# A third row pair in the seven-product form, and a new order of units, in the output product of a fused encoder layer

## The chip, the cores and the metric

The kernel runs on one core of a Trainium2 chip, in one launch. The metric is the device time of that core in microseconds (us). The engines that matter here are TensorE (PE in the profile, with its weight loads as PEld), VectorE (DVE), ScalarE (ACT) and the DMA queue that SyncE feeds (SPq). They run in parallel, each takes its own instructions strictly in order, and they meet only at semaphores.

## The reference

One layer of a hybrid encoder on 256 rows (tokens) of width 2048 in float32. The stage that is changed is the third line, `merged @ w_out`, a 256x2048 by 2048x2048 product that is added to `x`:

```
y_conv = conformer_conv_branch(...)          # ends in h @ w_conv_out
y_mla  = mla_branch(...)                     # ends in o @ w_mla_out
merged = gates[:, :, 0, :] * y_conv + gates[:, :, 1, :] * y_mla
x = x + merged @ w_out[l]
x = x + memory_cross_attention(rms_norm(x, norm_mem_g[l]), rms_norm(mem, mem_norm_g[l]), ...)
x = x + squared_relu_mlp(rms_norm(x, norm_ffn_g[l]), w_ff1[l], w_ff2[l])
```

## The kernel before

**Precision.** Each float32 operand is split into a rounded "high" part and the rest, the "low" part. A block product is three matmuls: high by high, high by low, low by high. For a block of activations of 128 rows of K by 128 tokens, against 512 columns of weights, that is three matmuls of 128x512 (`product`).

**Units.** Weights come in units of two K blocks by 512 columns (512 KB). A ring of four raw slots (`raw`) and a ring of four split slots (`w_both`, high and low) carry them. For unit u, SyncE loads the raw slot once the low part of unit u-4 is made (`load`). ScalarE makes the high part (`hi`, 128x1024) once the load has landed and TensorE has released unit u-4 (`used`). VectorE makes the low part (`lo`, 128x1024) after `hi`. TensorE then runs the unit. In the loops of ScalarE and VectorE over k, the unit that is split is k + LEAD with LEAD = 3, and everything else in step k stands around it. A plain unit is four block products, 12 matmuls.

**Seven for eight.** The 2048 output columns are taken as two chunk pairs (p = 0 and 1, 1024 columns each), K as eight row pairs of two blocks. For one row pair, one pair of chunks and the two token halves, the plain way takes 2 x 2 x 2 = 8 block products. Two units of the same row pair (the "left" unit, chunk 0, and the "right" unit, chunk 1) can instead be taken in seven products, in the manner of Strassen and Winograd. The left unit then carries two products, the right unit one, and the other four run later from sums of weight blocks and sums of activation blocks. VectorE makes the weight sums from both raw slots (`w_sums`, three instructions that each wait for the one before). ScalarE splits off their high part in two halves (`ws_high`), VectorE the low part (`ws_low`, two halves). There is one `w_sum` buffer, so each row pair's sums wait for the low parts of the one before. Of the right unit only the second half is split (`hi_second`, `lo_second`). The sums of activations are made once, from the turned merged rows (`h_sums`, `h_low`), and serve both chunk pairs. The later products run behind unit 13 and behind unit 14 of the 16.

**Order around the stage.** The list `FF2_ORDER` gives (chunk, first K block) of each unit; `LEFT` and `RIGHT` are the positions of the left and right units, so that before the change two row pairs of eight, at positions 7, 8 and 11, 12, take seven products. The convolution output product (`U_COUT`, c = 2 and 3) runs before the stage. In it the merged rows of the first three chunks are turned (transposed on TensorE, `turn`) and split (`turn_out`, `turn_low`). The fourth is turned behind unit 3 of pair 0. In pair 1 TensorE turns the new `xres` behind units 1 and 12. A turn takes 8 small matmuls.

Of the kernel before, what the change touches and what calls it, by code (L numbers as in the profile page):

```python
# [211 lines left out]
def build(nc, x, mem, positions, norm_mix_g, w_in, b_gate, conv_w, conv_b, conv_ln_g, conv_ln_b,  # L212
# [9 lines left out]
    with ExitStack() as ctx:  # L222
# [75 lines left out]
        ws_hi = ((ws_a0_hi, ws_b0_hi), (ws_a1_hi, ws_b1_hi))  # L298
        ws_lo = ((ws_a0_lo, ws_b0_lo), (ws_a1_lo, ws_b1_lo))
# [389 lines left out]
        def _(act):  # L689
# [273 lines left out]
            for c in range(2, CH):  # L963
                for k in range(UPC):
# [3 lines left out]
                    if c == 2 and k == 4:  # L968
                        h_high(2)

            def out_squares(c):
# [3 lines left out]
                chunk_squares(sq_res, xres[:, :, NC * c:NC * (c + 1)], c, SS_MEM + TT * c)  # L975

            for p in range(2):
                for k in range(FF2_UNITS):
                    if k == 12:
                        y_out(OUT, p, 0)  # L980
                    if k + LEAD in RIGHT:
# [1610 lines left out]
```

## Time and profile before

| | |
|---|---|
| Time, median of 3 runs | 1596.12 us (1596.04 to 1596.23) |
| Profiled execution: its time, its span | 1596.36 us, 1594.1 us |
| Busy over the span | PE 99%, PEld 84%, DVE 82%, ACT 56% |
| Chain that ended last | PE 98% |
| In pair 0 of the stage (755 to 799 us) | PE 44.0 of 44 us, DVE 35.8, ACT 22.3 |
| In pair 1 of the stage (799 to 843 us) | PE 44.0 of 44 us, DVE 36.6, ACT 25.8 |

The span is the time from the first to the last instruction; the run's own time is 2.3 us longer. The duration of a matmul in the trace (389 ns) is a latency. Matmuls overlap, and their spacing is what a row of them costs. The same holds of VectorE and ScalarE to a smaller degree: an instruction of 1.22 us is followed by the next after 1.14 us.

### The profile page before, as it was taken

Reading aid. Unit: us, or ns where it says so; the run is one execution under the profiler, and the core shown is the slowest. Engines: PE = TensorE matmul, PEld = TensorE weight load, DVE = VectorE, ACT = ScalarE, POOL = GpSimd, SP = SyncE. Lnnn points to the kernel's source line nnn. Section 1 sums busy time; section 2 is a strip of 40 time slices with the busy share of each in tenths; the row PEclk is TensorE's granted clock in tenths of the full one; section 3 lists DMA queues with packets and bytes.
Section 4 is the critical chain, followed back from the end, with each engine's and each line's share of the span. In section 5 each row is a group of like instructions: output and inputs, shape, how many; then the busy total and the mean of one; then the engine's idle time right before and its main releaser. Section 6 shows DMA issues by size and latency. Waiting matters only on the chain.

```text
span 1594.1 us, 22178 instructions
## 1 busy us (share of the span) xinstructions
PE 1582.9 (99%) x7915; PEld 1343.4 (84%) x7915; DVE 1299.3 (82%) x1741; ACT 900.2 (56%) x1133; POOL 94.5 (6%) x174
## 2 busy tenths in 40 slices
PE   9999999999999999999999999999999999999997
PEld 8888888888888888888888888888888888888886
DVE  5588999999998998786887787886779676968687
ACT  6444456555555556754566666455655565546655
POOL 6500010000000000000000000000000000000001
PEclk9999999999999999999999999999999999999999
DMA  7666655655555666657664676888678867987694
GB/s 254 203 187 186 194 158 178 174 181 172 182 177 174 209 200 185 197 177 249 212 195 145 179 230 186 279 258 291 181 256 267 266 217 219 286 259 237 207 293 147
DMA packets 169581, 336.68 MB, mean 211 GB/s; under 512 B 10377, under 2 KB 23297, under 8 KB 169089
## 3 DMA queue, kind: packets, MB, share of 16 engines
q1 hardware_dynamic: 164608, 324.84, 64.4%
q0 software_dynamic: 4864, 10.80, 3.1%
q8 instruction: 50, 0.82, 0.2%
q14 instruction: 27, 0.22, 0.0%
q10 hardware_dynamic: 32, 0.01, 0.0%
HBM read 326.16 MB, written 2.10 MB: 206 GB/s over the span
## 4 chain that ended last, share of the span: by engine, by line
PE 98%; DVE 0%; ACT 0%; issue 0%; ACTq 0%; POOL 0%; POOLq 0%; DVEq 0%
PE ps L2508 15%; PE ps L1937 12%; PE ps L1939 12%; PE ps L1938 12%; PE ps L2217 9%; PE ps L2215 9%; PE ps L2216 9%; PE ps L2510 7%; PE ps L1950 1%; PE ps L2126 1%; PE ps L2335 1%; PE ps L2121 1%; PE ps L2104 1%; PE ps L2106 1%; PE ps L2105 1%; PE ps L2160 1%
## 5 line engine op out<-in xcount | busy, mean ns | idle before, releaser
L695 ACT ACTIVATE w_both<-raw 128x1024 fp32r<-128x1024 f32 x524 | 553.2, 1059 | 498.7 <-PE ps L1939 178.5
L1188 DVE TENSOR_TENSOR w_both<-raw,w_both 128x1024 fp32r<-128x1024 f32 x524 | 637.3, 1222 | 201.6 <-ACT w_both L695 199.9
L2508 PE MATMUL ps<-a_both,w_both 128*128 128x512 f32 x1024 | 321.6, 395 | 0.0
L1937 PE MATMUL ps<-w_both,a_both 128*128 128x512 f32 (+1 forms) x636 | 251.4, 395 | 0.1
L1939 PE MATMUL ps<-w_both,a_both 128*128 128x512 f32 (+1 forms) x636 | 247.1, 388 | 0.0
L1938 PE MATMUL ps<-w_both,a_both 128*128 128x512 f32 (+1 forms) x636 | 246.9, 388 | 0.0
L2510 PEld LDWEIGHTS ps<-a_both,w_both 128*128 128x128 f32 x1024 | 192.4, 188 | 45.4
L1249 DVE SCALAR_TENSOR_TENSOR acc<-hconv,cwk,acc 128x256 f32<-128x256 f32 x464 | 201.1, 486 | 7.7 <-PE ps L2160 7.6
L2510 PE MATMUL ps<-a_both,w_both 128*128 128x256 f32 x1024 | 201.2, 278 | 0.0
L2215 PE MATMUL ps<-w_both,c_hi 128*128 128x512 f32 x414 | 161.4, 390 | 0.0
L2216 PE MATMUL ps<-w_both,c_hi 128*128 128x512 f32 x414 | 161.1, 389 | 0.0
L2217 PE MATMUL ps<-w_both,c_lo 128*128 128x512 f32 x414 | 161.1, 389 | 0.0
L2508 PEld LDWEIGHTS ps<-a_both,w_both 128*128 128x128 f32 x1024 | 156.2, 189 | 0.3
L1939 PEld LDWEIGHTS ps<-w_both,a_both 128*128 128x128 f32 x636 | 119.4, 188 | 24.5
L1937 PEld LDWEIGHTS ps<-w_both,a_both 128*128 128x128 f32 x636 | 119.5, 188 | 23.2 <-DVE a_both L1209 0.3
L1938 PEld LDWEIGHTS ps<-w_both,a_both 128*128 128x128 f32 x636 | 119.6, 188 | 22.5
L2217 PEld LDWEIGHTS ps<-w_both,c_lo 128*128 128x128 f32 x414 | 77.7, 188 | 16.3
L2216 PEld LDWEIGHTS ps<-w_both,c_hi 128*128 128x128 f32 x414 | 77.7, 188 | 16.0
L2215 PEld LDWEIGHTS ps<-w_both,c_hi 128*128 128x128 f32 x414 | 77.7, 188 | 15.7
L1797 DVE TENSOR_TENSOR t_lo<-t_raw,t_hi 128x2048 fp32r<-128x2048 f32 x31 | 71.0, 2291 | 12.9 <-ACT t_hi L1090 12.7
L1090 ACT ACTIVATE t_hi<-t_raw 128x2048 fp32r<-128x2048 f32 x31 | 59.1, 1907 | 3.0 <-DVE t_raw L1792 3.0
L675 POOL DMA_DIRECT2D xres<-m_sum x7 | 8.4, 1197 | 820.0 <-DVE xres L1631 820.0
(418 smaller groups left out, 2208.4 us busy)
## 6 DMA issues: line engine op xcount, KB each, us to landing
raw<-in_w_ff_dram SPq DMA_DIRECT2D x225, 512.0 KB, 4.6
raw<-in_w_in_dram SPq DMA_DIRECT2D x137, 512.0 KB, 4.2
t_raw<-in_w_ff_dram SPq DMA_DIRECT2D x31, 1024.0 KB, 7.2
raw<-in_w_mla_out_dram SPq DMA_DIRECT2D x32, 512.0 KB, 4.3
raw<-in_w_conv_out_dram SPq DMA_DIRECT2D x32, 512.0 KB, 4.5
raw<-in_w_out_dram SPq DMA_DIRECT2D x32, 512.0 KB, 4.4
raw<-in_w_ukv_dram SPq DMA_DIRECT2D x16, 512.0 KB, 3.8
raw<-in_w_xkv_dram SPq DMA_DIRECT2D x16, 512.0 KB, 3.8
```

The costliest lines, as they stand in the source:

```text
L695: act.activation(whi[:, s, :], raw[:, s, :], ACT.Copy).then_inc(hi_ready, 1)
L1188: dve.tensor_tensor(wlo[:, s, :], raw[:, s, :], whi[:, s, :].bitcast(F32), ALU.subtract).then_inc(lo_ready, 1)
L1249: ins = dve.scalar_tensor_tensor(out=to, in0=h[:, tap:tap + SEQ], scalar=cwk[:, tap:tap + 1], in1=to, op0=ALU.mult, op1=ALU.add)
L1797: dve.tensor_tensor(t_lo[j % SLOTS][:], t_raw[j % SLOTS][:], t_hi[j % SLOTS][:].bitcast(F32), ALU.subtract).then_inc(t_lo_ready, 1)
L1937: pe.matmul(sum_, x_hi[:, k0 + k, tok], w_hi, start=(first and k == 0), stop=False)
L1938: pe.matmul(sum_, x_hi[:, k0 + k, tok], w_lo, start=False, stop=False)
L1939: mm = pe.matmul(sum_, x_lo[:, k0 + k, tok], w_hi, start=False, stop=(last and k == kts - 1))
L2215: pe.matmul(ps[:, bank, :], x_hi, w_hi, start=first, stop=False, skip_group_check=True)
L2216: pe.matmul(ps[:, bank, :], x_hi, w_lo, start=False, stop=False, skip_group_check=True)
L2217: return pe.matmul(ps[:, bank, :], x_lo, w_hi, start=False, stop=last, skip_group_check=True)
L2508: pe.matmul(both, whi[:, s, cols[n]], a_both[:, :, k0 + k, :], start=(first and k == 0), stop=False)
L2510: mm = pe.matmul(ps[:, b0 + b + n, 0:SEQ], wlo[:, s, cols[n]], a_hi[:, k0 + k, :], start=False, stop=(last and k == 1))
```

## The change

A third row pair takes the seven-product form in both chunk pairs. A new list `OUT_ORDER` replaces `FF2_ORDER` for this stage; left units stand at 4, 8 and 11, right units at 5, 9 and 12. `sum_high` and `sum_low` say at which step k the high and low parts of the weight sums are made. The third row pair's activation sums come from new code (`h3_sums`, a high and a low part) in the convolution output product, its weight sums get buffers in the idle `a_both` region, and a scratch of squares moves to another region. The convolution's own pair keeps the old list.

```diff
@@ -137,6 +137,12 @@
              (1, 10), (0, 12), (0, 2), (1, 2), (0, 14), (1, 12), (1, 14))
 FF2_UNITS = len(FF2_ORDER)
 LEFT, RIGHT = (7, 11), (8, 12)
+OUT_ORDER = ((0, 6), (0, 8), (1, 6), (1, 8), (0, 0), (1, 0), (0, 10), (1, 10), (0, 2),
+             (1, 2), (0, 12), (0, 4), (1, 4), (0, 14), (1, 12), (1, 14))
+OUT_LEFT, OUT_RIGHT = (4, 8, 11), (5, 9, 12)
+OUT_WS_HIGH = (2, 6, 10)
+OUT_WS_LOW = {2: (0, 1), 3: (0, 0), 6: (1, 1), 7: (1, 0), 10: (2, 1), 11: (2, 0)}
+OUT_PLANS = ((OUT_ORDER, OUT_LEFT, OUT_RIGHT, OUT_WS_HIGH, OUT_WS_LOW),) * 2
 ONES_BANK, LAST_BANK = 4, 5
 FF2_BANKS = ((2, 0), (2, 6))
 V_BANK, K_BANK = 4, 6
@@ -168,6 +174,16 @@
 TURN_MRG = {(2, 1): (0,), (2, 6): (1,), (3, 3): (2,)}


+def sums_before(p, m):
+
+    return 3 * m + (6 + 9 * p if p >= 0 else 0)
+
+
+def halves_before(p, m):
+
+    return 2 * m + (4 + 6 * p if p >= 0 else 0)
+
+
 def pair_of(n):

     return (n + 1) % 2
@@ -244,6 +260,8 @@
         sq_mem = at(o + KS + KS // 2, "sq_mem", [P, TT, NC])
         fin = at(o, "fin", [P, TT, D])
         fin_g = at(o + KS, "fin_g", [P, D])
+        ws_a2_hi, ws_b2_hi, ws_a2_lo, ws_b2_lo = (
+            at(o + at_byte, f"ws_third{n}", [P, 2 * NC], F32R) for n, at_byte in enumerate((8192, 12288, 24576, 28672)))
         sq_fin = at(o + KS + nbytes([P, D]), "sq_fin", [P, TT, NC])

         o = c_base = cursor[0]
@@ -295,8 +313,10 @@
...
-        ws_hi = ((ws_a0_hi, ws_b0_hi), (ws_a1_hi, ws_b1_hi))
-        ws_lo = ((ws_a0_lo, ws_b0_lo), (ws_a1_lo, ws_b1_lo))
+        ws_hi = ((ws_a0_hi, ws_b0_hi), (ws_a1_hi, ws_b1_hi), (ws_a2_hi, ws_b2_hi))
+        ws_lo = ((ws_a0_lo, ws_b0_lo), (ws_a1_lo, ws_b1_lo), (ws_a2_lo, ws_b2_lo))
+        h3_hi = at(o + 12288, "h3_hi", [P, 4, P], F32R)
+        h3_sum, h3_lo = at(o + 14336, "h3_sum", [P, 4, P]), at(o + 14336, "h3_lo", [P, 4, P], F32R)
@@ -516,7 +538,7 @@
             sp.wait_ge(h_made, 4)
             sp.dma_start(xres[:], x_v).then_inc(res_landed, 16)
             for p in range(2):
-                for i, (c, k) in enumerate(FF2_ORDER):
+                for i, (c, k) in enumerate(OUT_PLANS[p][0]):
                     n = 2 * p + c
                     load(U_WOUT + FF2_UNITS * p + i, 0, w_out[:, k:k + 2, NC * n:NC * (n + 1)])
             for hp in range(2):
@@ -967,18 +989,21 @@
...
+                    if c == 2 and k == 7:
+                        act.wait_ge(h3_made, 5)
+                        act.activation(h3_hi[:], h3_sum[:], ACT.Copy).then_inc(h3_hi_ready, 1)
...
-                chunk_squares(sq_res, xres[:, :, NC * c:NC * (c + 1)], c, SS_MEM + TT * c)
...
+                chunk_squares(sq_out, xres[:, :, NC * c:NC * (c + 1)], c, SS_MEM + TT * c)
+
+            for p, (_, _, right, sum_high, _) in enumerate(OUT_PLANS):
                 for k in range(FF2_UNITS):
                     if k == 12:
                         y_out(OUT, p, 0)
-                    if k + LEAD in RIGHT:
+                    if k + LEAD in right:
                         hi_second(U_WOUT + FF2_UNITS * p + k + LEAD, 0)
                     else:
                         hi(U_WOUT + FF2_UNITS * p + k + LEAD)
@@ -989,8 +1014,8 @@
                         turn_out(T_X1 + c, a_hi, 4 * c, V_NMEM)
                     if p and k in (4, 8):
                         out_squares(k // 4 - 1)
-                    if k in (5, 10):
-                        ws_high(OUT, p, k // 10)
+                    if k in sum_high:
+                        ws_high(OUT, p, sum_high.index(k))
                     if k == 14:
                         y_out(OUT, p, 1)

@@ -1510,26 +1535,40 @@
...
+            def h3_sums():
+
+                dve.wait_ge(turn_hi, 2 * (T_MRG + 1) + 1)
+                x11, x12, x21, x22 = (ps[:, 6, SEQ * k + P * t:SEQ * k + P * (t + 1)] for t, k in ((0, 0), (0, 1), (1, 0), (1, 1)))
+                s1, s2, s3, s4 = (h3_sum[:, i, :] for i in range(4))
+                dve.tensor_copy(s4, x21).then_inc(h3_made, 1)
+                dve.wait_ge(h3_made, 1)
+                dve.tensor_tensor(s1, s4, x22, ALU.add).then_inc(h3_made, 1)
+                dve.tensor_tensor(s3, x11, s4, ALU.subtract).then_inc(h3_made, 1)
+                dve.wait_ge(h3_made, 3)
+                dve.tensor_tensor(s2, s1, x11, ALU.subtract).then_inc(h3_made, 1)
+                dve.wait_ge(h3_made, 4)
+                dve.tensor_tensor(s4, x12, s2, ALU.subtract).then_inc(h3_made, 1)
+
             def w_sums(g, p, m, u, r=0, left_at=LEFT, b=late):

-                done = 6 * p + 3 * m + 18
+                done = sums_before(p, m)
...
-                wait(dve, ws_lo_ready, g * 8 + (4 * p + 2 * m + 12))
+                wait(dve, ws_lo_ready, halves_before(p, m))
...
-                dve.wait_ge(ws_made, g * 12 + (done + 1))
+                dve.wait_ge(ws_made, done + 1)
                 dve.tensor_tensor(t2, right[:, NC:], t1, ALU.subtract).then_inc(ws_made, 1)
-                dve.wait_ge(ws_made, g * 12 + (done + 2))
+                dve.wait_ge(ws_made, done + 2)
                 dve.tensor_tensor(t4, left[:, NC:], t2, ALU.subtract).then_inc(ws_made, 1)
@@ -1589,10 +1628,15 @@
                         dve.wait_ge(h_lifted, 1)
                         for n in range(4):
                             h_sums(OUT, n, turned_blocks, h_sum[:, 3, :, :])
+                    if (c, k) == (2, 6):
+                        h3_sums()
                     for n in TURN_MRG.get((c, k), ()):
                         turn_low(T_MRG + n, c_lo, c_hi, 4 * n)
                     if (c, k) == (2, 5):
                         h_low(OUT)
+                    if (c, k) == (3, 1):
+                        dve.wait_ge(h3_hi_ready, 1)
+                        dve.tensor_tensor(h3_lo[:], h3_sum[:], h3_hi[:].bitcast(F32), ALU.subtract).then_inc(h3_lo_ready, 1)
                 n = N_COUT + c
                 p = pair_of(n)
                 dve.wait_ge(used, U_COUT + UPC * (c + 1))
@@ -1630,14 +1674,14 @@
...
-            for p in range(2):
+            for p, (_, left, right, _, sum_low) in enumerate(OUT_PLANS):
                 u = U_WOUT + FF2_UNITS * p
                 for k in range(FF2_UNITS):
                     i = k + LEAD
-                    if i in LEFT:
+                    if i in left:
                         dve.wait_ge(chunk_out, N_WOUT + 2 * p)
-                        w_sums(OUT, p, LEFT.index(i), u)
-                    if i in RIGHT:
+                        w_sums(OUT, p, left.index(i), u, left_at=left)
+                    if i in right:
                         lo_second(u + i, 0)
                     else:
                         lo(u + i)
@@ -1646,10 +1690,8 @@
                     if p and k in TURN_X1:
                         c = TURN_X1.index(k)
                         turn_low(T_X1 + c, a_lo, a_hi, 4 * c, V_NMEM)
-                    if k in (5, 6):
-                        ws_low(OUT, p, 0, 6 - k)
-                    if k in (10, 11):
-                        ws_low(OUT, p, 1, 11 - k)
+                    if k in sum_low:
+                        ws_low(OUT, p, *sum_low[k])
                     if k == 14:
                         dve.wait_ge(p4_done, p + 2)
                         dve.wait_ge(res_landed, 16)
@@ -2234,44 +2281,46 @@
...
-                for i, (c, k) in enumerate(FF2_ORDER):
+                for i, (c, k) in enumerate(order):
...
+                    if i in left:
+                        m = left.index(i)
+                        mm = product(ONES_BANK, *hidden(2 * m, 0), *slot(i, 0), first=(m == 0), last=(m == end))
+                        if m == end:
                             mm.then_inc(y_step, 1)
                         product(banks[0], *hidden(2 * m + 1, 0), *slot(i, 1)).then_inc(used, 1)
...
+                    elif i in right:
+                        m = right.index(i)
                         pe.wait_ge(h_lo_ready, sums)
+                        if m == 2:
+                            pe.wait_ge(h3_lo_ready, 1)
                         product(banks[1], *combined(3, m), *slot(i, 1), first=banks[1] not in begun).then_inc(used, 1)
...
+                    if i == left[end] + 2:
+                        pe.wait_ge(ws_lo_ready, halves_before(p, end) + 1)
                         pe.wait_ge(y_copied, g * 4 + (2 * p + 7))
-                        for m in range(2):
-                            mm = product(ONES_BANK, *combined(1, m), *weight_sum(2, m), last=(m == 1))
+                        for m in range(end + 1):
+                            mm = product(ONES_BANK, *combined(1, m), *weight_sum(2, m), last=(m == end))
                         mm.then_inc(y_step, 1)
-                        for m in range(2):
-                            mm = product(banks[0] + 1, *hidden(2 * m + 1, 1), *weight_sum(3, m), last=(m == 1))
+                        for m in range(end + 1):
+                            mm = product(banks[0] + 1, *hidden(2 * m + 1, 1), *weight_sum(3, m), last=(m == end))
                         mm.then_inc(p4_done, 1)
-                    if i == LEFT[1] + 3:
-                        pe.wait_ge(ws_lo_ready, g * 8 + (4 * p + 16))
+                    if i == left[end] + 3:
+                        pe.wait_ge(ws_lo_ready, halves_before(p, end) + 2)
                         pe.wait_ge(y_copied, g * 4 + (2 * p + 8))
-                        for m in range(2):
-                            mm = product(ONES_BANK, *combined(0, m), *weight_sum(0, m), last=(m == 1))
+                        for m in range(end + 1):
+                            mm = product(ONES_BANK, *combined(0, m), *weight_sum(0, m), last=(m == end))
                         mm.then_inc(y_step, 1)
-                        for m in range(2):
-                            mm = product(LAST_BANK, *combined(2, m), *weight_sum(1, m), first=(m == 0), last=(m == 1))
+                        for m in range(end + 1):
+                            mm = product(LAST_BANK, *combined(2, m), *weight_sum(1, m), first=(m == 0), last=(m == end))
                         mm.then_inc(p7_done, 1)
@@ -2301,13 +2350,15 @@


             for p in range(2):
+                plan = OUT_PLANS[p][:3]
+
                 def out_waits(i, k):

                     if p == 0:
                         pe.wait_ge(turn_lo, 2 * splits_before(T_MRG) + k // 2 + 1)
                     if i in (0, 2):
                         pe.wait_ge(chunk_out, N_WOUT + 2 * p - 1 + i // 2)
-                    if i == LEFT[0]:
+                    if i == plan[1][0]:
                         pe.wait_ge(mixed, 3 * (p + 1))

                 def out_turns(i):
```

On VectorE, pair 0 of the stage, the rows of before begin with the last four low parts ahead of the first row pair's sums (`c_lo` is the turned fourth chunk, `w_sum` a row pair's sums, `w_both` a unit's low part, `ws` the low part of sums):

```order
L1188 TENSOR_TENSOR w_both<-raw,w_both 128x1024 x4
L1204 TENSOR_TENSOR c_lo<-ps,c_hi 128x512 x2
L1523 TENSOR_TENSOR w_sum<-raw 128x1024
L1526 TENSOR_TENSOR w_sum<-raw,w_sum 128x512
L1528 TENSOR_TENSOR w_sum<-raw,w_sum 128x512
L1188 TENSOR_TENSOR w_both<-raw,w_both 128x1024
L1194 TENSOR_TENSOR w_both<-raw,w_both 128x512
L1533 TENSOR_TENSOR ws_72<-w_sum,ws_71 128x1024
L1188 TENSOR_TENSOR w_both<-raw,w_both 128x1024
L1533 TENSOR_TENSOR ws_70<-w_sum,ws_69 128x1024
L1188 TENSOR_TENSOR w_both<-raw,w_both 128x1024
L1523 TENSOR_TENSOR w_sum<-raw 128x1024
```

In the changed kernel VectorE has, from the same `c_lo` on (lines L1229, L1572, L1213, L1562, L1565, L1567 and L1219 are `turn_low`, `ws_low`, `lo`, the three of `w_sums`, and `lo_second`):

```order
L1229 TENSOR_TENSOR c_lo<-ps,c_hi 128x512 x2
L1572 TENSOR_TENSOR ws_74<-w_sum,ws_73 128x1024
L1213 TENSOR_TENSOR w_both<-raw,w_both 128x1024
L1562 TENSOR_TENSOR w_sum<-raw 128x1024
L1565 TENSOR_TENSOR w_sum<-raw,w_sum 128x512
L1567 TENSOR_TENSOR w_sum<-raw,w_sum 128x512
L1213 TENSOR_TENSOR w_both<-raw,w_both 128x1024
L1219 TENSOR_TENSOR w_both<-raw,w_both 128x512
L1572 TENSOR_TENSOR ws_b_lo<-w_sum,ws_b_hi 128x1024
L1213 TENSOR_TENSOR w_both<-raw,w_both 128x1024
L1572 TENSOR_TENSOR ws_78<-w_sum,ws_77 128x1024
L1562 TENSOR_TENSOR w_sum<-raw 128x1024
```

The low part of unit 11, which stood three rows behind the second set of sums, now stands behind the third set, and two full sets and four low parts of sums lie between the start of the pair and it.

On ScalarE in pair 0 of before (`w_both` is the high part of a unit, `ws` that of sums):

```order
L709 ACTIVATE c_hi<-ps 128x512 x2
L695 ACTIVATE w_both<-raw 128x1024
L702 ACTIVATE w_both<-raw 128x512
L932 ACTIVATE ws_71<-w_sum 128x1024
L932 ACTIVATE ws_69<-w_sum 128x1024
L695 ACTIVATE w_both<-raw 128x1024 x3
```

and in the changed kernel:

```order
L731 ACTIVATE c_hi<-ps 128x512 x2
L717 ACTIVATE w_both<-raw 128x1024 x2
L724 ACTIVATE w_both<-raw 128x512
L954 ACTIVATE ws_b_hi<-w_sum 128x1024
L954 ACTIVATE ws_77<-w_sum 128x1024
L717 ACTIVATE w_both<-raw 128x1024 x2
L724 ACTIVATE w_both<-raw 128x512
```

The high parts of the second row pair's sums now stand ahead of the high part of unit 10.

## Rows read from the trace of the kernel before

**Rows 1.** Head of the page: the span, and the granted clock in 40 slices.

```profile
span 1594.1 us, 22178 instructions
...
PEclk9999999999999999999999999999999999999999
```

**Rows 2.** Windows: start and end, their length, busy time by engine (instructions), clock, DMA.

```profile
core 0: us, PE busy (x) PEld busy (x) DVE busy (x) ACT busy (x) POOL busy (x), PEclk, DMA share, GB/s
...
0.00:5.00 5.00, 3.46 (x15) 3.23 (x15) 0.00 (x0) 1.49 (x2) 3.29 (x27) 1.00 0.52 145
...
755.00:799.00 44.00, 44.00 (x200) 36.54 (x199) 35.80 (x35) 22.27 (x25) 0.00 (x0) 1.00 0.67 211
799.00:843.00 44.00, 44.00 (x205) 36.63 (x204) 36.57 (x39) 25.82 (x39) 0.00 (x0) 1.00 0.61 191
```

**Rows 3.** All waits of TensorE in the whole run (total, times, longest).

```profile
PE ps L1966 <- POOL stat L579: 1.5, 1, 1.5
```

**Rows 4.** Timeline of TensorE: start, duration; starts of units and turns.

```profile
755.16 0.39 PE L2215 MATMUL ps<-w_both,c_hi 128*128 128x512 f32 x1
...
766.04 1.04 PE L1950 MATMUL ps<-ident,rows 128*128 128x128 f32 x8
...
782.57 0.39 PE L2215 MATMUL ps<-w_both,c_hi 128*128 128x512 f32 x1
...
804.45 0.48 PE L2215 MATMUL ps<-w_both,c_hi 128*128 128x512 f32 x1
```

**Rows 5.** Timeline of VectorE in pair 0: start, duration, idle before and its releaser.

```profile
767.31 1.29 DVE L1204 TENSOR_TENSOR c_lo<-ps,c_hi 128x512 fp32r<-128x512 f32 x2 [1.41 <-ACT c_hi L709]
768.51 1.22 DVE L1523 TENSOR_TENSOR w_sum<-raw 128x1024 f32<-128x1024 f32 x1
...
771.10 1.22 DVE L1188 TENSOR_TENSOR w_both<-raw,w_both 128x1024 fp32r<-128x1024 f32 x1
772.24 0.68 DVE L1194 TENSOR_TENSOR w_both<-raw,w_both 128x512 fp32r<-128x512 f32 x1
772.84 1.22 DVE L1533 TENSOR_TENSOR ws<-w_sum,ws 128x1024 fp32r<-128x1024 f32 x1
...
780.29 1.22 DVE L1188 TENSOR_TENSOR w_both<-raw,w_both 128x1024 fp32r<-128x1024 f32 x1
...
782.02 1.22 DVE L1188 TENSOR_TENSOR w_both<-raw,w_both 128x1024 fp32r<-128x1024 f32 x1
```

**Rows 6.** Timeline of ScalarE in pair 0, same columns.

```profile
771.22 2.01 ACT L932 ACTIVATE ws<-w_sum 128x1024 fp32r<-128x1024 f32 x2 [0.67 <-DVE w_sum L1528]
773.13 1.04 ACT L695 ACTIVATE w_both<-raw 128x1024 fp32r<-128x1024 f32 x1
...
785.48 1.07 ACT L695 ACTIVATE w_both<-raw 128x1024 fp32r<-128x1024 f32 x1 [0.83 <-DMA raw<-in_w_out_dram]
...
788.84 1.06 ACT L695 ACTIVATE w_both<-raw 128x1024 fp32r<-128x1024 f32 x1 [0.75 <-DMA raw<-in_w_out_dram]
```

**Rows 7.** Timeline of ScalarE in pair 1, behind the first turn.

```profile
804.29 1.57 ACT L712 ACTIVATE a_both<-ps,vec 128x256 fp32r<-128x256 f32 x4 [2.04 <-PE ps L1950]
805.74 1.08 ACT L695 ACTIVATE w_both<-raw 128x1024 fp32r<-128x1024 f32 x1
```

**Rows 8.** Timeline of VectorE in pair 1, behind the first turn.

```profile
805.17 1.66 DVE L1209 SCALAR_TENSOR_TENSOR a_both<-ps,vec,a_both 128x256 fp32r<-128x256 f32 x4 [1.66 <-ACT a_both L712]
```

**Rows 9.** Timeline at the start: TensorE's first plain matmul behind a low part.

```profile
10.25 1.23 DVE L1188 TENSOR_TENSOR w_both<-raw,w_both 128x1024 fp32r<-128x1024 f32 x1
...
11.63 0.47 PE L1937 MATMUL ps<-w_both,a_both 128*128 128x512 f32 x1
```

**Rows 10.** Timeline of VectorE in the convolution output product.

```profile
716.26 0.41 DVE L1588 COPY h_sum<-ps 128x256 f32<-128x256 f32 x1
...
739.28 1.23 DVE L1188 TENSOR_TENSOR w_both<-raw,w_both 128x1024 fp32r<-128x1024 f32 x1 [1.49 <-ACT w_both L695]
```

**Rows 11.** Timeline of ScalarE at the stage's first unit.

```profile
748.52 1.06 ACT L695 ACTIVATE w_both<-raw 128x1024 fp32r<-128x1024 f32 x1 [2.48 <-DMA raw<-in_w_out_dram]
```

More of the change, by code:

```diff
@@ L331, in build @@
         xq_part = at(o, "xq_part", [P, 2, SEQ])
+        sq_out = at(o, "sq_out", [P, TT, NC])
         ff_row = at(o, "ff_row", [P, 2, CPB, SEQ])
@@ L417, in build @@
         h_lifted, h_made, h_hi_ready, h_lo_ready = (sem(n) for n in ("h_lifted", "h_made", "h_hi_ready", "h_lo_ready"))
+        h3_made, h3_hi_ready, h3_lo_ready = (sem(n) for n in ("h3_made", "h3_hi_ready", "h3_lo_ready"))
         ws_made, ws_hi_ready, ws_lo_ready = (sem(n) for n in ("ws_made", "ws_hi_ready", "ws_lo_ready"))
@@ L1631, in add_chunk @@
                 dve.tensor_tensor(cols, ps[:, bank:bank + 2, :], cols, ALU.add).then_inc(chunk_out, 1)
-            for p in range(2):
+            for p, (_, left, right, _, sum_low) in enumerate(OUT_PLANS):
                 u = U_WOUT + FF2_UNITS * p
@@ L2217, in product, with seven_pair @@
                 return pe.matmul(ps[:, bank, :], x_lo, w_hi, start=False, stop=last, skip_group_check=True)
-            def seven_pair(g, p, u, r, banks, first_use, between, sums, b=late, x_hi=c_hi, x_lo=c_lo):
+            def seven_pair(g, p, u, r, banks, first_use, between, sums, b=late, x_hi=c_hi, x_lo=c_lo, plan=(FF2_ORDER, LEFT, RIGHT)):
+                order, left, right = plan
+                end = len(left) - 1
                 def hidden(k, t):
@@ L2225, in combined @@
                 def combined(n, m):
+                    if m == 2:
+                        return h3_hi[:, n, :], h3_lo[:, n, :]
                     return b.h_hi[:, n, m, :], b.h_lo[:, n, m, :]
@@ L2236, in seven_pair @@
                 begun = set()
-                for i, (c, k) in enumerate(FF2_ORDER):
+                for i, (c, k) in enumerate(order):
                     pe.wait_ge(lo_ready, u + i + 1 + r)
                     first_use(i, k)
-                    if i in LEFT:
-                        m = LEFT.index(i)
-                        mm = product(ONES_BANK, *hidden(2 * m, 0), *slot(i, 0), first=(m == 0), last=(m == 1))
-                        if m == 1:
+                    if i in left:
+                        m = left.index(i)
+                        mm = product(ONES_BANK, *hidden(2 * m, 0), *slot(i, 0), first=(m == 0), last=(m == end))
+                        if m == end:
                             mm.then_inc(y_step, 1)
                         product(banks[0], *hidden(2 * m + 1, 0), *slot(i, 1)).then_inc(used, 1)
-                    elif i in RIGHT:
-                        m = RIGHT.index(i)
+                    elif i in right:
+                        m = right.index(i)
                         pe.wait_ge(h_lo_ready, sums)
+                        if m == 2:
+                            pe.wait_ge(h3_lo_ready, 1)
                         product(banks[1], *combined(3, m), *slot(i, 1), first=banks[1] not in begun).then_inc(used, 1)
@@ L2253, in seven_pair @@
                             for t in range(TT):
-                                ends = n == 1 and (i == 15 or (i == LEFT[1] + 2 and t == 0))
+                                ends = n == 1 and (i == 15 or (i == left[end] + 2 and t == 0))
                                 mm = product(banks[c] + t, *hidden(k + n, t), *slot(i, n), first=banks[c] + t not in begun, last=ends)
```

8 lines of the change are left out of this document (3 added, 5 removed).

## The prediction

> **What bounds the kernel now.** The head of the page gives a span of 1594.1 us with TensorE's clock at full in every slice [rows 1]. The list of waits holds one wait of TensorE in the whole run, 1.5 us at the start [rows 3]. In both halves of the stage, 755 to 799 and 799 to 843 us, TensorE is busy for all 44.00 us [rows 2]. So TensorE's issue is the bound, and a matmul removed is worth its spacing, not its 0.39 us. From the first matmul of pair 0 (755.16) to the turn behind unit 3 (766.04) are 48 matmuls [rows 4]: 10.88 / 48 = 0.2267 us each.
>
> The reader should then ask what keeps TensorE fed. VectorE is busy for 35.8 of 44 us in pair 0 and 36.6 in pair 1, ScalarE for 22.3 and 25.8 [rows 2]. VectorE has 7 to 8 us to spare, and it is not spread evenly. It makes the low part of unit 11 from 780.29 to 781.51 [rows 5], and TensorE starts unit 11 at 782.57 [rows 4]: 1.06 us of cover, right behind the second row pair's sums. That is where more sums hurt first.
>
> **The change, part by part.**
>
> *Matmuls removed.* The third row pair takes seven products for eight in each chunk pair, so three matmuls less twice: 6 x 0.2267 = 1.36 us. This is the whole possible gain, 0.09% of the time. The number and size of the loads stay.
>
> *Work added on VectorE in each pair.* Spacing is read from starts [rows 5]. The three sums take 771.10 - 768.51 = 2.59 us. A low part is 782.02 to the next at 1.14 (as 771.10 to 772.24), a half low part 772.84 - 772.24 = 0.60. The third row pair adds 2.59 + 2 x 1.14 and turns one low part into a half one, -0.54: +4.33 us a pair. The total still fits in 44 us. What counts is where it falls.
>
> *Order, pair 0.* The turn behind unit 3 stays at 766.04, and VectorE's chain hangs on it, at 767.31 [rows 4, 5]. From there the changed VectorE has, in its order: turned chunk 1.20 (to 768.51); low sums 1.14 (769.65); unit 7 1.14 (770.79); second sums 2.59 (773.38); unit 8 1.14, unit 9 0.60 (775.12); low sums 1.14 (776.26). Then unit 10. Its high part stands on ScalarE behind the two high parts of the second sums. ScalarE takes those two in 773.13 - 771.22 = 1.91 us [rows 6], beginning 0.05 behind the sums, and a high part is usable about 1.09 later: 773.43 + 1.91 + 1.09 = 776.43. VectorE goes on: unit 10 (777.57), low sums (778.71), third sums 2.59 (781.30), unit 11 ready 1.22 later at 782.52.
>
> What TensorE wants: its turn ends at 766.04 + 0.80 = 766.84 (eight transposes of some 0.10). Units 4 to 10 are now 6 + 3 + 12 + 12 + 6 + 3 + 12 = 54 matmuls, 12.24 us, so unit 11 is wanted at 779.08. It is 3.44 us late. On the way TensorE will have waited 0.2 to 0.4 us at unit 8 (wanted 774.32, ready 774.60) and about 1 us at unit 10; these are part of the 3.44. A wake adds something: at the start a matmul follows the low part's end at 11.48 by 0.15 us [rows 9]. Pair 0 loses 3.6 us.
>
> *Order, pair 1.* TensorE's unit 2 starts at 804.45 behind the turn [rows 4]. Units 2 to 10 are 78 matmuls, 17.69 us: unit 11 is wanted at 822.14, on the clock of before. ScalarE is free of the turned chunk at 805.74 [rows 7]. Behind it come half a high part 0.53 (an estimate, half of the full one), two high sums 1.91, and unit 6's high part 1.09: 809.27. VectorE's own chain from 805.17 [rows 8] (the turned chunk 1.66 less the usual overlap of 0.08, then 0.60 and 1.14) is there sooner, so it waits. Then unit 6 and low sums (811.55), unit 7 (812.69), second sums (815.28), unit 8, unit 9, low sums (818.16), a wait for unit 10's high part (815.28 + 0.05 + 1.91 + 1.09 = 818.33), unit 10 and low sums (820.61), third sums (823.20), unit 11 at 824.42. It is 2.28 us late, 2.4 with the wake. Behind unit 11 both pairs recover: 18 late matmuls in place of 12 now follow unit 13 and again unit 14 (1.36 us more cover each), and no sums are left to make.
>
> *Loads.* The third sums need the raw slot of unit 12, whose load follows the low part of unit 8 (774.60). ScalarE waited for a load until 785.48, that is 3.97 us behind the low part that freed its slot (781.51), and for a later one in the burst until 788.84, 5.6 us behind the low part of unit 13 (782.02 + 1.22) [rows 5, 6]. The first case gives 778.57, just under the 778.71 at which VectorE comes; the other 780.20, 1.5 us late in each pair. The load of unit 12 is the first after a pause, so it is nearest to the first: I put 0.1 us a pair, and keep 0 and 1.5 as the ends.
>
> *Activation sums and the rest.* Five small VectorE instructions on 128x128 are not in the trace. The same step on 128x256 takes 0.41 us [rows 10], so five cost under 2.3 us, and above 0. They stand in a stretch where VectorE waits for ScalarE, 1.49 us ahead of one low part [rows 10], and TensorE wants that unit 5 us later. They push back the loads by up to that much; the stage's first high part waits for its load until 748.52 [rows 11], so is usable as a low part at some 750.8 or 753, while TensorE wants it at 755.16. Price nothing; with that cover gone, up to 2.3 us once. By the Trainium skill (VectorE: DVE Perf Modes, the section on the TRN2 errata) a float32 tensor_tensor takes (N + 151) / 0.96 ns, 291 ns at 128 columns, so five take 1.5 us by that page; its 691 ns at 512 agree with the 0.69 of the sums here. The added high parts on ScalarE and the moved scratch lie beside TensorE's work: ScalarE is under 60% busy [rows 2].
>
> **Sum.** -1.36 + 3.6 + 2.4 + 0.2 = +4.8 us. The profiled run has a span of 1594.1 and a time of 1596.36, 0.24 above the median of 1596.12. Against its own time the sum gives 1601.2, against the median 1600.9. I predict 1600.9 us, +0.30%.
>
> **The rivals.** A change of under 0.2% (3.2 us) cannot be told from none here.
>
> *Cover holds (not slower).* One mechanism: VectorE's chain up to unit 11 hides. It decides from a total of waits under 1.36 + 3.2 = 4.55 us, so both chains would have to be some 0.8 us shorter than the rows add up to. Without any wait the time is 1596.12 - 1.36 = 1594.8. For it: 7 us of idle VectorE in each pair. Against it: the idle time lies ahead of the turn and behind unit 13, and the chain from 767.31 is made of spacings from this very stretch. Chance of ending within 0.2%: 0.15.
>
> *Later loads.* Each pair's third sums wait 1.5 us for unit 12's slot: 1600.9 + 2 x 1.4 = 1603.7. For it: the 5.6 us above. Against it: those were the third load in a burst. Chance 0.08.
>
> *The clock falls.* If the waits at units 10 and 11 made the granted clock drop from 2.4 to 1.2 GHz, each plain unit run so would cost another 2.7 us; one or two units in each pair give 1606 to 1612. Against it: the slices and windows stand at 1.00, also the first 5 us with the 1.5 us wait [rows 1 to 3]. The Trainium skill (TensorE: Matmul & The Clock Gate, on what is actually happening) says that idleness brings the half rate back. Chance 0.03.
>
> *More than the removed matmuls is gained* (faster by over 0.2%): nothing in the rows gives 3.2 us, chance 0.02.
>
> The forecast, waits of 5.2 to 7.2 us in all, has 0.72. Its own range is 1600 to 1602. The 8-in-10 range has to reach into the held cover and into later loads: 1597.5 to 1603.2. Faster 0.02, same 0.15, slower 0.83.
>
> **What would show it.** In the changed profile TensorE should have 2.0 to 2.5 us of idle ahead of the left unit 11 in each pair, some 1 us ahead of unit 10 in pair 0, and waits for VectorE's low part (line `lo`) that sum to about 6 us; six matmuls less; VectorE without a gap from the turned chunk to unit 11 except one small wait for ScalarE. Pair 0 should be near 3 us longer and pair 1 near 1.8. I am wrong if TensorE's wait list is still empty in the stage, if the third sums wait for a DMA for over a microsecond, or if the activation sums make TensorE wait ahead of the stage.

## The result, and the profile after

The changed kernel takes 1604.01 us (median of 6 runs, 1601.44 to 1604.78) against 1596.17 us (1595.77 to 1596.44). The ratio is 1.0047, 95% interval [1.0036, 1.0058]: slower by 7.8 us. The direction was forecast, the size was not. 1600.9 was predicted, and the range ended at 1603.2, 0.8 us short.

The profiled execution has a span of 1601.0 us, 6.9 us more than before, and a time of 1603.27 us. All waits of TensorE in it, against [rows 3]:

```profile
PE ps L2257 <- DVE w_both L1213: 5.1, 3, 2.3
PE ps L2008 <- POOL stat L601: 1.5, 1, 1.5
```

Three waits for VectorE's low part (L1213) are new. The windows of the stage, against [rows 2], show where they fall, and one thing more (the last line is the second window in the kernel before):

```profile
755.00:799.00 44.00, 40.85 (x182) 32.94 (x182) 38.54 (x38) 22.96 (x26) 0.00 (x0) 1.00 0.64 206
799.00:850.00 51.00, 48.97 (x217) 40.12 (x216) 43.13 (x47) 28.23 (x41) 0.00 (x0) 0.97 0.54 173
...
799.00:850.00 51.00, 51.00 (x251) 42.94 (x250) 40.50 (x45) 32.01 (x54) 0.00 (x0) 1.00 0.56 175
```

TensorE is no longer busy throughout, VectorE is busier, and in the second window the granted clock is 0.97. The timeline of TensorE has the start of the stage, its turn and the pauses, against [rows 4]:

```profile
754.83 0.39 PE L2257 MATMUL ps<-w_both,c_hi 128*128 128x512 f32 x1
...
765.72 1.03 PE L1992 MATMUL ps<-ident,rows 128*128 128x128 f32 x8
...
776.27 0.39 PE L2259 MATMUL ps<-w_both,h_lo 128*128 128x512 f32 x1
...
777.43 0.50 PE L2257 MATMUL ps<-w_both,c_hi 128*128 128x512 f32 x1 [0.77 <-DVE w_both L1213]
...
780.06 0.39 PE L2259 MATMUL ps<-w_both,c_lo 128*128 128x512 f32 x1
...
782.74 0.50 PE L2257 MATMUL ps<-w_both,c_hi 128*128 128x512 f32 x1 [2.29 <-DVE w_both L1213]
...
825.33 0.39 PE L2259 MATMUL ps<-w_both,c_lo 128*128 128x512 f32 x1
...
827.75 0.50 PE L2257 MATMUL ps<-w_both,c_hi 128*128 128x512 f32 x1 [2.03 <-DVE w_both L1213]
...
829.39 0.63 PE L2257 MATMUL ps<-w_both,h_hi 128*128 128x512 f32 x1
829.82 0.63 PE L2258 MATMUL ps<-w_both,h_hi 128*128 128x512 f32 x1
```

A pause is read here as the distance of two starts less the usual 0.23. Ahead of unit 10 in pair 0 it is 777.43 - 776.27 - 0.23 = 0.93 us, ahead of unit 11 it is 2.45, and in pair 1 ahead of unit 11 it is 2.19. The first matmul behind a pause is 0.11 us longer to its successor. With two small ones (0.23 at unit 8 of pair 0, 0.13 at unit 10 of pair 1) and five times 0.11 the pauses sum to 6.5 us. Behind 829 us the matmuls are 0.43 us apart instead of 0.23. The windows there say why (columns as in [rows 2]):

```profile
828.00:829.00 1.00, 1.00 (x5) 0.79 (x5) 1.00 (x2) 1.00 (x2) 0.00 (x0) 1.00 0.21 14
829.00:830.00 1.00, 1.00 (x4) 0.80 (x3) 1.00 (x2) 1.00 (x2) 0.00 (x0) 0.53 0.81 193
830.00:831.00 1.00, 1.00 (x5) 0.71 (x4) 1.00 (x2) 0.02 (x1) 0.00 (x0) 0.50 0.98 272
831.00:832.00 1.00, 1.00 (x7) 1.00 (x6) 1.00 (x2) 0.00 (x0) 0.00 (x0) 0.50 0.94 320
832.00:833.00 1.00, 1.00 (x6) 0.91 (x5) 0.83 (x1) 0.81 (x1) 0.00 (x0) 0.77 1.02 352
```

The granted clock is at 0.50 (1.2 GHz) from 829 to past 832 us, a little over 1 us behind the end of the pause of pair 1. The matmuls and transposes there are 1.7 us later than their usual spacings add up to. So -1.36 + 6.5 + 1.7 = +6.8 us, against a span that is 6.9 us longer.

The six runs sort by their mean granted clock: 1601.44 us at 0.998, 1603.27 and 1603.53 at 0.997, 1604.49, 1604.55 and 1604.78 at 0.996. That looks like none, one or two such stretches in a run, and the median lies between the runs with one and those with two. Only the run of 1603.27 us has a trace; for the others the stretches are inferred from the time and the mean clock.

VectorE's chain in pair 0, against [rows 5]:

```profile
766.98 1.29 DVE L1229 TENSOR_TENSOR c_lo<-ps,c_hi 128x512 fp32r<-128x512 f32 x2 [1.15 <-ACT c_hi L731]
768.19 1.22 DVE L1572 TENSOR_TENSOR ws<-w_sum,ws 128x1024 fp32r<-128x1024 f32 x1
769.32 1.22 DVE L1213 TENSOR_TENSOR w_both<-raw,w_both 128x1024 fp32r<-128x1024 f32 x1
770.46 1.22 DVE L1562 TENSOR_TENSOR w_sum<-raw 128x1024 f32<-128x1024 f32 x1
...
776.15 1.23 DVE L1213 TENSOR_TENSOR w_both<-raw,w_both 128x1024 fp32r<-128x1024 f32 x1
777.30 1.22 DVE L1572 TENSOR_TENSOR ws<-w_sum,ws 128x1024 fp32r<-128x1024 f32 x1
778.87 1.23 DVE L1562 TENSOR_TENSOR w_sum<-raw 128x1024 f32<-128x1024 f32 x1 [0.35 <-DMA raw<-in_w_out_dram]
...
781.47 1.22 DVE L1213 TENSOR_TENSOR w_both<-raw,w_both 128x1024 fp32r<-128x1024 f32 x1
```

Unit 11's low part ends at 782.69 us. The chain of the prediction gave 782.52, on a clock 0.33 us later (the stage starts at 754.83 for 755.16). So it comes 0.5 us later than forecast. VectorE stands idle for 0.35 us ahead of the third sums, put down to unit 12's load, but not all of that is the load's: where no load is waited for, as in the first kernel below, the third sums still start 1.35 us behind the start of the low sums and not the 1.14 that the prediction took. Here it is 1.57, so the load adds about 0.2 us.

### The profile page after: what moved, and what is told of

It reads as the page before. It is cut to its first block, busy times and chain, and to the rows that moved or that the text cites. A ratio compares the mean times of both kernels' runs of the same rounds, so it can differ in the third digit from the quotient of the medians.

```text
span 1601.0 us, 22193 instructions
## 1 busy us (share of the span) xinstructions
PE 1584.6 (99%) x7909; PEld 1342.8 (84%) x7909; DVE 1308.8 (82%) x1757; ACT 903.0 (56%) x1138; POOL 94.1 (6%) x174
## 4 chain that ended last, share of the span: by engine, by line
PE 96%; DVE 2%; ACT 1%; issue 1%; DMA 0%; ACTq 0%; POOL 0%; DVEq 0%; POOLq 0%
PE ps L2559 15%; PE ps L1979 12%; PE ps L1981 12%; PE ps L1980 12%; PE ps L2257 9%; PE ps L2258 9%; PE ps L2259 9%; PE ps L2561 7%; PE ps L1992 1%; PE ps L2168 1%; PE ps L2386 1%; PE ps L2163 1%; PE ps L2146 1%; PE ps L2148 1%; PE ps L2147 1%; PE ps L2202 1%
## 5 line engine op out<-in xcount | busy, mean ns | idle before, releaser
L1213 DVE TENSOR_TENSOR w_both<-raw,w_both 128x1024 fp32r<-128x1024 f32 x522 | 634.5, 1222 | 196.4 <-ACT w_both L717 193.8
L2257 PE MATMUL ps<-w_both,c_hi 128*128 128x512 f32 x402 | 157.5, 392 | 5.2 <-DVE w_both L1213 5.1
L2259 PE MATMUL ps<-w_both,c_lo 128*128 128x512 f32 x402 | 156.6, 390 | 0.0
L2258 PE MATMUL ps<-w_both,c_hi 128*128 128x512 f32 x402 | 156.5, 389 | 0.0
L2257 PEld LDWEIGHTS ps<-w_both,c_hi 128*128 128x128 f32 x402 | 75.6, 188 | 23.0 <-DVE w_both L1213 7.7
L2258 PEld LDWEIGHTS ps<-w_both,c_hi 128*128 128x128 f32 x402 | 75.5, 188 | 15.1
```

The lines of the kernel that those rows point to most:

```text
L1213: dve.tensor_tensor(wlo[:, s, :], raw[:, s, :], whi[:, s, :].bitcast(F32), ALU.subtract).then_inc(lo_ready, 1)
L2257: pe.matmul(ps[:, bank, :], x_hi, w_hi, start=first, stop=False, skip_group_check=True)
L2258: pe.matmul(ps[:, bank, :], x_hi, w_lo, start=False, stop=False, skip_group_check=True)
L2259: return pe.matmul(ps[:, bank, :], x_lo, w_hi, start=False, stop=last, skip_group_check=True)
```

## The experiments

One theory was tested against its rivals. **Chain:** VectorE's order of work up to unit 11 sets the pauses of TensorE (the expectations call this the VectorE theory), and the clock falls behind the long ones in a part of the runs (the clock theory). Against it stood that the loads set the pauses, that the new order of units or the activation sums do, or that the fall of the clock has to do with something else in the changed code.

**One pair at a time.** In the first kernel pair 1 has the plan of before, in the second pair 0; the counts of semaphores follow.

```diff
-OUT_PLANS = ((OUT_ORDER, OUT_LEFT, OUT_RIGHT, OUT_WS_HIGH, OUT_WS_LOW),) * 2
+OUT_PLANS = ((OUT_ORDER, OUT_LEFT, OUT_RIGHT, OUT_WS_HIGH, OUT_WS_LOW),
+             (FF2_ORDER, LEFT, RIGHT, (5, 10), {5: (0, 1), 6: (0, 0), 10: (1, 1), 11: (1, 0)}))
```

> Only chunk pair 0 takes the third row pair, in the new order; pair 1 keeps the order and the two row pairs of before. Three matmuls less, -0.7 us. If VectorE's chain up to unit 11 sets the pauses, pair 0 pauses as in the changed kernel (0.3 + 1.0 + 2.6 us with the wakes, 3.9 in all) and pair 1 not at all: +3.2 us against before while the clock stays up, 1599.4. If a pause of over 2 us can halve the clock once for some 3.4 us, a share of the runs is 1.7 us longer (1601.1) and the runs fall on these two levels only. If the slowdown came from something common to both pairs (the activation sums ahead of the stage, the moved scratch), it would be near the full +7.

Measured: 1600.55 us (9 runs; before 1596.07), ratio 1.0027 [1.0017, 1.0037]. Four runs lie at 1599.41 to 1599.70 (clock 0.998 or 0.999), five at 1600.55 to 1601.27 (0.997). The profiled execution is one of the first four. The pause ahead of its unit 11, and VectorE's low sums and third sums:

```profile
780.07 0.39 PE L2260 MATMUL ps<-w_both,c_lo 128*128 128x512 f32 x1
782.50 0.50 PE L2258 MATMUL ps<-w_both,c_hi 128*128 128x512 f32 x1 [2.05 <-DVE w_both L1214]
...
777.29 1.22 DVE L1573 TENSOR_TENSOR ws<-w_sum,ws 128x1024 fp32r<-128x1024 f32 x1
778.64 1.23 DVE L1563 TENSOR_TENSOR w_sum<-raw 128x1024 f32<-128x1024 f32 x1
```

The pause is 2.20 us, for 2.45 in the changed kernel: the third sums do not wait for a load here. The ones at units 8 and 10 are 0.23 and 0.93 us as there, 3.7 us in all with three times 0.11 (3.9 expected).

> Only chunk pair 1 takes the third row pair in the new order; pair 0 is as before. By VectorE's chain: -0.7 + 2.5 us of pauses ahead of units 10 and 11 of pair 1 = +1.9 us, 1598.0 with the clock up and 1599.7 with one drop; no third level. The two pairs' losses add up to that of the changed kernel. A common cause would show here as well as in the other pair's run and the two would not add up.

Measured: 1599.06 us (11 runs), ratio 1.0019 [1.0010, 1.0028]. Six runs lie at 1597.98 to 1599.06, five at 1599.65 to 1600.02; the two groups are only 0.6 us apart here, and one run of the upper has the mean clock 0.998 of the lower, so the split is less sharp than in the first kernel. Its one long pause, in the timeline of TensorE:

```profile
821.95 0.39 PE L2260 MATMUL ps<-w_both,c_lo 128*128 128x512 f32 x1
824.38 0.50 PE L2258 MATMUL ps<-w_both,c_hi 128*128 128x512 f32 x1 [2.04 <-DVE w_both L1214]
```

It is 2.20 us, the 2.19 of the changed kernel's pair 1. The lower groups stand 3.5 and 2.3 us above before (their means), and these add up to 5.8; the changed kernel's one run with the clock up is 5.3 above. The losses are each pair's own. The upper groups lie 1.3 and 1.4 us above the lower ones, where 1.7 was expected.

**VectorE's sums made narrow.** The three instructions of a set of sums work on 32 of 512 columns a block, in the first kernel in the third set alone, in the second in every set but pair 0's first. Most of the sums are left out, so the output is incomplete; one of the three is shown.

```diff
+w = 32 if p >= 0 and m == 2 else NC
...
-dve.tensor_tensor(t2, right[:, NC:], t1, ALU.subtract).then_inc(ws_made, 1)
+dve.tensor_tensor(t2[:, 0:w], right[:, NC:NC + w], t1[:, 0:w], ALU.subtract).then_inc(ws_made, 1)
...
# second kernel: w = 32 if p >= 0 and (m or p) else NC
```

> The changed kernel, but the three instructions of the third row pair's weight sums work on 32 of their 512 columns a block, so the sums (and the output) are incomplete; semaphores, loads, low and high parts and all matmuls are unchanged. VectorE theory: the chain loses about 2.0 us ahead of unit 11, which then is some 0.4 us late in each pair; what is left is units 8 and 10 (1.4 us in pair 0, 0.4 in pair 1), no pause reaches 2 us, the clock does not fall: -1.4 + 2.7 = about +1.3 us, 1597.5. Load theory (the third sums wait for unit 12's slot): the pause ahead of unit 11 stays at over 1 us, +3 us or more.

Measured: 1597.31 us, 11 runs within 1597.12 to 1597.70, ratio 1.0008 [0.9999, 1.0017]. The pauses at unit 11 fall to 0.22 and 0.42 us, the one at unit 10 of pair 0 stays at 0.94. The load theory wanted over 1 us to stay at unit 11. Nothing spreads the runs any more.

> As the one before, but all weight sums of both pairs are narrow except pair 0's first (the output is incomplete). VectorE theory: no pause over 0.2 us is left, the clock stays up in every run, and the time is that of the removed matmuls alone: 1596.1 - 1.3 = 1594.8, all runs on one level. If ScalarE's order (high parts of the second sums ahead of unit 10's) sets the pause at unit 10 whenever it comes, 1 us stays in pair 0.

Measured: 1596.22 us (1595.67 to 1597.23), ratio 1.0001 [0.9992, 1.0010]: 1.4 us over what was expected. The pause at unit 10 is gone, one at unit 11 is left. VectorE and then TensorE in pair 0:

```profile
771.11 1.22 DVE L1213 TENSOR_TENSOR w_both<-raw,w_both 128x1024 fp32r<-128x1024 f32 x1
...
777.74 0.23 DVE L1563 TENSOR_TENSOR w_sum<-raw 128x64 f32<-128x64 f32 x1 [1.17 <-DMA raw<-in_w_out_dram]
```

```profile
778.69 0.39 PE L2260 MATMUL ps<-w_both,c_lo 128*128 128x512 f32 x1
779.61 0.50 PE L2258 MATMUL ps<-w_both,c_hi 128*128 128x512 f32 x1 [0.54 <-DVE w_both L1213]
```

The third sums now wait for the load of unit 12, whose slot came free with unit 8's low part at 772.33 and which is there 5.4 us later. In pair 1 they wait 1.54 us for theirs. So the loads were not the main cause, but they are the next bound close behind: with VectorE's sums nearly free, pauses of 0.69 and 0.43 us, each with its 0.11, give back the 1.36 us of matmuls.

**The order of units alone.**

```diff
+SPREAD_ORDER = ((0, 6), (0, 8), (1, 6), (1, 8), (0, 4), (1, 4), (0, 10), (1, 10), (0, 0),
+                (1, 0), (0, 12), (0, 2), (1, 2), (0, 14), (1, 12), (1, 14))
...
-OUT_PLANS = ((OUT_ORDER, OUT_LEFT, OUT_RIGHT, OUT_WS_HIGH, OUT_WS_LOW),) * 2
+OUT_PLANS = ((SPREAD_ORDER, (8, 11), (9, 12), (6, 10), {6: (0, 1), 7: (0, 0), 10: (1, 1), 11: (1, 0)}),
+             (SPREAD_ORDER, (8, 11), (9, 12), (6, 10), {6: (0, 1), 7: (0, 0), 10: (1, 1), 11: (1, 0)}))
```

> The new order of units with only two row pairs in the seven-product form, at positions 8, 9 and 11, 12; positions 4 and 5 are plain units of the third row pair. As many matmuls as before. If the third set of sums ahead of unit 11 is what hurts, two sets this close together cost little: at most 0.3 us of pause in all, 1596.1 to 1596.4, one level. If the new order of units (left and right units closer to each other) hurts by itself, two pauses of about a microsecond or more stay, +2 us.

Measured: 1596.83 us (1596.62 to 1597.50), ratio 1.0005 [0.9996, 1.0014]. The pauses are 0.24 and 0.23 us at unit 11, each with its 0.10 to 0.11. That is 0.7 us in all, more than the 0.3 expected: two sets of sums this close have no cover left, but cost little beside three. The activation sums of the third row pair are still made in this kernel, unused. The median is 0.8 us above before, so beyond the pauses they cost nothing that can be seen.

**A pause alone, in the kernel before.** Idle VectorE instructions in pair 1, ahead of unit 11's low part; two, three and four of them.

```diff
...
 w_sums(OUT, p, LEFT.index(i), u)
+if p and i == LEFT[1]:
+    for n in range(2):
+        dve.tensor_tensor(idle_out[n][:], c_hi[:, 0:4, :].bitcast(F32), c_lo[:, 0:4, :].bitcast(F32), ALU.add)
```

> The kernel before, with two idle VectorE instructions of 128x1024 (they add two tiles into an unused region) in pair 1 behind the second row pair's sums, ahead of unit 11's low part. 2 x 1.14 us less the 1.06 us of cover and plus the wake: one pause of 1.3 to 1.4 us of TensorE, 1597.5. Clock theory: a pause this short does not halve the clock, all runs on one level. Without such an effect of length the share of slow runs is the same in all three pause kernels.

> As the one before with three idle instructions: one pause of 2.5 us, 1598.6 with the clock up. Clock theory: as in the changed kernel's pair 1, about half of the runs are 1.7 us longer (1600.3), two levels. If the drop came from something else in the changed kernel (its matmuls on sums, its loads), all runs stay at 1598.6.

> As the one before with four idle instructions: one pause of 3.6 us, 1599.7 with the clock up. Clock theory: nearly all runs drop, median 1601.4; if the price is the same stretch at half clock whatever the pause, the step between levels stays 1.7 us.

| idle instructions | pause, us | runs, us | runs with the lower clock | ratio |
|---|---|---|---|---|
| 2 | 1.15 | 1597.32 (1597.19 to 1597.90) | 0 of 11 | 1.0008 [0.9999, 1.0017] |
| 3 | 2.28 | 1598.89 (1598.44 to 1600.34) | 2 of 11 (1600.29, 1600.34) | 1.0019 [1.0010, 1.0028] |
| 4 | 3.41 | 1601.73 (1600.95 to 1602.57) | 5 of 5 | 1.0036 [1.0022, 1.0049] |

The pause is read from the one profiled execution of each kernel, the lower clock from the mean clock of each run: 0.996 or 0.997, where the other runs here and all of before have 0.998 or 0.999.

The pause of the third kernel, in the timeline of TensorE, and the doubled spacing behind it:

```profile
825.06 0.39 PE L2221 MATMUL ps<-w_both,c_lo 128*128 128x512 f32 x1
828.70 0.50 PE L2219 MATMUL ps<-w_both,c_hi 128*128 128x512 f32 x1 [3.25 <-DVE w_both L1189]
829.04 0.53 PE L2220 MATMUL ps<-w_both,c_hi 128*128 128x512 f32 x1
829.36 0.63 PE L2221 MATMUL ps<-w_both,c_lo 128*128 128x512 f32 x1
829.79 0.63 PE L2219 MATMUL ps<-w_both,c_hi 128*128 128x512 f32 x1
```

A pause of TensorE is enough to lower the clock; nothing else of the change is in these kernels. The expected half of the runs at a pause of 2.3 us was 2 of 11. The two lie 1.5 us above the mean of the other nine.

**The same pauses cut otherwise.** Only the places of the second sums' low (and, in the second kernel, high) parts differ.

```diff
-OUT_WS_LOW = {2: (0, 1), 3: (0, 0), 6: (1, 1), 7: (1, 0), 10: (2, 1), 11: (2, 0)}
+OUT_WS_LOW = {2: ((0, 1),), 3: ((0, 0),), 6: ((1, 1), (1, 0)), 10: ((2, 1),), 11: ((2, 0),)}
...
# second kernel: OUT_WS_HIGH = (2, 7, 10), and 7: ((1, 1), (1, 0)) in place of 6
```

> The changed kernel with the order of three VectorE instructions changed in each pair: both low parts of the second row pair's sums ahead of unit 10's low part (before: one ahead, one behind). Nothing is added or removed, so by VectorE's chain unit 11 comes when it came: the pauses sum to the same 6.5 us, but part of the one at unit 11 moves to unit 10 (pair 0 about 2.0 and 1.4, pair 1 about 1.3 and 1.1 instead of 0.9 and 2.4, 0.1 and 2.2). Clock theory: no pause is over 2.1 us, so most runs stay up: median 1601.5. If the clock follows the sum of pauses rather than the longest, the runs stay on 1603 to 1605 as in the changed kernel.

Measured: 1601.03 us, 6 runs within 1600.61 to 1601.65, ratio 1.0032 [1.0019, 1.0044]. TensorE's two long pauses of pair 0 in it:

```profile
776.37 0.39 PE L2260 MATMUL ps<-w_both,h_lo 128*128 128x512 f32 x1
778.43 0.50 PE L2258 MATMUL ps<-w_both,c_hi 128*128 128x512 f32 x1 [1.68 <-DVE w_both L1213]
...
781.06 0.39 PE L2260 MATMUL ps<-w_both,c_lo 128*128 128x512 f32 x1
782.50 0.50 PE L2258 MATMUL ps<-w_both,c_hi 128*128 128x512 f32 x1 [1.05 <-DVE w_both L1213]
```

They are 1.83 and 1.21 us, in pair 1 1.03 and 0.96. With the small ones all pauses sum to 5.8 us, 0.7 less than in the changed kernel, and no run has the lower clock. That speaks against the sum of the pauses as what counts: pair 0 alone has 3.6 us of them here, with the 0.11s, and its clock fell in 0 of 6 runs, while the kernel with pair 0 alone has 3.7 us there, one pause of 2.20 among them, and its clock fell in 5 of 9.

> The opposite: ScalarE makes unit 10's high part ahead of the high parts of the second row pair's sums, and VectorE both low parts of those sums behind unit 10's low part. By the chain the pause at unit 10 goes (it was ScalarE's order) and the one at unit 11 takes it over: 3.4 us in pair 0, 2.5 us in pair 1, same sum. Clock theory: pair 0 drops in every run and pair 1 in some, median 1603.3 to 1604.8, none at 1601.5.

Measured: 1604.68 us (1603.11 to 1605.23), ratio 1.0052 [1.0039, 1.0066]. In pair 0 the pause at unit 10 is gone and there is one at unit 11; windows in and behind it:

```profile
779.22 0.39 PE L2260 MATMUL ps<-w_both,c_lo 128*128 128x512 f32 x1
783.50 0.80 PE L2258 MATMUL ps<-w_both,c_hi 128*128 128x512 f32 x1 [3.89 <-DVE w_both L1213]
...
782.00:783.00 1.00, 0.00 (x0) 0.00 (x0) 1.00 (x2) 0.66 (x1) 0.00 (x0) 0.57 0.00 0
...
784.00:786.00 2.00, 2.00 (x6) 1.52 (x5) 2.00 (x3) 1.78 (x3) 0.00 (x0) 0.50 0.67 145
786.00:788.00 2.00, 2.00 (x7) 1.52 (x6) 2.00 (x3) 0.15 (x1) 0.00 (x0) 0.50 0.97 297
788.00:789.00 1.00, 1.00 (x4) 0.81 (x3) 0.65 (x2) 0.91 (x1) 0.00 (x0) 0.52 0.96 363
```

It is 4.05 us (3.4 expected; the third sums wait 1.13 us for their load here). The clock fell within the pause, between 782 and 783 us, and stayed at 0.50 until close to 789. The matmuls behind the pause are 2.7 us later than their usual spacings, not 1.7: the price of a fall is not always the same. Pair 1, with a pause of 2.46 us, kept its clock in this execution. The median lies in the range expected, but not by the sizes expected: the pause and the fall of pair 0 both cost more. The pause at unit 10 was expected to go since ScalarE's order made it. That is not shown. The kernel also moves a low part of sums behind unit 10 on VectorE, which is 1.14 us; in the changed kernel VectorE started unit 10's low part only 0.2 us later than its own spacings give. Between these two kernels, which differ in the places of a few instructions alone, lie 3.7 us, about 1.3 of them in pauses and the rest in the clock.

## Why the prediction was wrong

- **Matmuls removed, -1.36 us:** TensorE has six matmuls less (7915 before, 7909 after), and the account of the span closes with that figure.
- **The chains:** right. Pair 0 was given 3.6 us of pauses and pair 1 2.4, and 0.2 for the loads, 6.2 in all; the trace has 3.9 and 2.5, 6.5. The loads took about 0.2 us in pair 0 and nothing in pair 1, as much in all as forecast. The sum did not have the 0.11 us behind each of five pauses, nor 0.2 us more between the low sums and the third sums in each pair; its wake was too large instead (0.15 us for the 0.05 from 782.69 to 782.74), so a little of the closeness is luck. The places (units 8, 10 and 11 of pair 0, 11 of pair 1) are those named. With the third sums narrow the pauses at unit 11 fall from 2.45 and 2.19 us to 0.22 and 0.42, and the single pairs show each pair's share.
- **The run without a fall of the clock** is 1601.44 us, 0.5 above the forecast of 1600.9.
- **The step that failed is the rival "The clock falls"**, with its chance of 0.03: the sum put at nothing what a pause costs beyond its own length. It was dismissed since the granted clock stood at 1.00 in all slices of before and in its first 5 us with a wait of 1.5 us. But the kernel before has no pause inside the stream of matmuls, so its rows could not speak for pauses of 2.2 and 2.45 us. The runs show that the clock falls behind such a pause in a part of the runs (5 of 6 for the changed kernel, 5 of 9 and 5 of 11 with one pair). Its price was also off. It was taken as whole plain units, 2.7 us each, in both pairs at once: 1606 to 1612. A stretch costs 1.7 us in the trace of the changed kernel, and 1.3 to 1.5 between the groups of runs of the kernels with one long pause, so one or two put the time at 1603 to 1605, in the gap between the forecast and that rival. A chance near one half a pair, at 1.7 us, would have given a range to 1605.
- **The rivals "Cover holds" and "Later loads"** did not occur. The second is true as the next bound: with narrow sums the wait for unit 12's load alone gives back the whole gain.
- **Activation sums and scratch, nothing:** in line with the run of the order alone. In the trace of the changed kernel the five instructions take 1.38 us together (729.82 to 731.20), 0.28 or 0.29 each, near the prediction's 1.5, and TensorE does not wait there.

What stays open: why a pause of some 2.2 us lowers the clock in about half of the runs of the one-pair kernels, and one of 2.28 us in 2 of 11 in the kernel before. That was not settled; the counts are small. The kernels differ in when a pause comes as well as in how long it is (the one with the second low sums early shifts its pauses too), and no run holds the length and moves the time. Why one fall cost 1.7 us and another 2.7 is open as well.

## What to carry to other kernels

Where TensorE is busy throughout, a saving of matmuls has to be checked against the engine that feeds it, unit by unit between two fixed points, and not against that engine's share of the span: VectorE had 7 us to spare in each pair and still came 3.9 us late for one unit (ready at 782.69 us; the turn's end at 766.52 and 54 matmuls give 778.76). Next, ask for the longest single pause that results, since a pause has a second price in the clock: the same work with its longest pause at 1.83 us in place of 2.45 ran 3 us faster, only 0.7 of it by less pause. And a kernel that never pauses says nothing on what a pause costs.

## What the hardware showed unexpectedly

- Behind one pause of TensorE of 1.15, 2.28 or 3.41 us in a stream at 2.4 GHz, the clock fell to 1.2 GHz in 0 of 11, 2 of 11 and 5 of 5 runs. By the Trainium skill (TensorE: Matmul & The Clock Gate, What's actually happening) idleness brings back the half rate; the traces of the changed kernel, of the pause of 3.41 us and of that of 4.05 us agree.
- The price of a fall was not the same each time: 1.7 us of later matmuls and transposes behind a pause of 2.19 us, and 2.7 behind one of 4.05 us, where the clock fell before the pause was over.
- At the lower clock a 128x512 matmul stood 0.43 us from the next, against 0.23.
- The first matmul behind a pause stood 0.33 to 0.34 us from the next also where the clock had stayed up, 0.11 more than usual.
